# A decode step with paged attention: chosen-row copies at other places of a fixed order, and later places for some waits of ScalarE and VectorE

## The reference, cut to what matters

```
kc, vc  = compress(rows[:, :, 0]), compress(rows[:, :, 1])   # 255 compressed keys and values of 4096 cached rows
o_cmp,p = cmp_attention(q, kc, vc)                           # softmax over the 255
sel     = top_k(importance of 64 blocks from p, 16)          # per KV head, first and newest blocks forced
o_slc   = softmax(q . keys of the 16 chosen blocks) . values # 15*64+1 = 961 rows
o_win   = softmax(q . last 512 keys) . values
out     = g0*o_cmp + g1*o_slc + g2*o_win
```

## Time and profile before

| | |
|---|---|
| median of 3 runs | 2246.21 us (2242.72 to 2254.63) |
| the profiled execution | 2249.45 us, span 2247.6 us |
| TensorE matmuls (PE), busy | 2016.1 us, 90% of the span |
| VectorE (DVE) | 915.7 us, 41% |
| ScalarE (ACT) | 707.9 us, 31% |
| GpSimd (POOL) | 629.6 us, 28% |
| DMA | 247.86 MB, 110 GB/s on average |
| granted TensorE clock | 0.955 of full speed |

### The profile page before, as it was taken

The page is one execution under the profiler, slowest core; times in us unless marked ns, Lnnn a source line. Parts: engine busy times, 40 slices in busy tenths (PEclk is TensorE's granted clock), DMA queues, the critical chain, the costliest instruction groups (busy, mean ns, idle before and its releaser), DMA issues. The chain is left out here.

```text
span 2247.6 us, 24649 instructions
## 1 busy us (share of the span) xinstructions
PE 2016.1 (90%) x9303; PEld 1372.5 (61%) x9303; DVE 915.7 (41%) x1821; ACT 707.9 (31%) x1297; POOL 629.6 (28%) x649
## 2 busy tenths in 40 slices
PE   8999999999999999999968778677687878899997
PEld 7888888888888877777634334333343434434442
DVE  0445355454510144444434344445353545432126
ACT  0233112332200032332335444445354544510013
POOL 0000000000020034343545465555565555240000
PEclk9999999999999999999979889898888998999999
DMA  5232222222232211111155253545454453564114
GB/s 202 67 101 77 85 85 77 94 75 85 77 111 76 93 61 57 38 57 38 54 177 146 76 159 90 179 121 165 134 144 142 139 155 119 164 234 155 75 75 151
DMA packets 71076, 247.86 MB, mean 110 GB/s; under 512 B 11220, under 2 KB 28832, under 8 KB 56768
## 3 DMA queue, kind: packets, MB, share of 16 engines
q1 hardware_dynamic: 38344, 139.10, 17.8%
q0 software_dynamic: 31360, 103.32, 15.7%
q10 hardware_dynamic: 1280, 4.23, 0.5%
HBM read 224.64 MB, written 21.96 MB: 110 GB/s over the span
## 5 line engine op out<-in xcount | busy, mean ns | idle before, releaser
L292 PE MATMUL pj<-xT,strips 128*128 128x260 f32 x2368 | 532.6, 384 | 6.4 <-DMA xT<-d_xT 6.4
L292 PEld LDWEIGHTS pj<-xT,strips 128*128 128x128 f32 x2368 | 445.9, 191 | 72.3 <-issue 6.3
L1835 ACT ACTIVATE big<-dtb 64x512 f32<-64x512 f32 x512 | 302.8, 591 | 314.6 <-PE dtb L1569 172.2
L792 PE MATMUL pj<-xT,strips 128*128 128x260 f32 x1216 | 292.0, 388 | 0.0
L1592 PE MATMUL dpH<-big,w 128*128 128x512 f32 x512 | 287.3, 658 | 0.4 <-DVE hs L1958 0.4
L792 PEld LDWEIGHTS pj<-xT,strips 128*128 128x128 f32 x1216 | 222.4, 190 | 59.8 <-issue 30.1
L1018 POOL MEMSET kbd<- 128x128 f32 x1 | 0.2, 205 | 635.4 <-POOLq L126 635.4
L1569 PEld LDWEIGHTS dtb<-const,xT 128*128 128x128 f32 x512 | 65.3, 150 | 181.5 <-issue 87.5
L1941 DVE TENSOR_TENSOR big<-big 128x512 f32<-128x512 f32 x128 | 88.3, 689 | 212.5 <-ACT big L1835 174.2
L1569 PE MATMUL dtb<-const,xT 128*128 128x128 f32 x512 | 84.7, 292 | 99.9 <-DVE KgT L1807 79.2
L1044 POOL TENSOR_SCALAR old<-old,rd 128x128 f32<-128x128 f32 (+3 forms) x116 | 122.2, 1068 | 166.6 <-DVE rd L1153 166.6
(11 more groups left out here) (311 smaller groups left out, 2402.1 us busy)
## 6 DMA issues: line engine op xcount, KB each, us to landing
strips<-d_w_in SPq DMA_DIRECT2D x60, 1024.0 KB, 5.3
xT<-d_w_out SPq DMA_DIRECT2D x16, 1024.0 KB, 7.5
d_win_sample<-Wt SPq DMA_DIRECT2D x8, 1024.0 KB
Xr<-d_w_out SPq DMA_DIRECT2D x8, 1024.0 KB, 10.1
Wt<-d_win SPq DMA_DIRECT2D x8, 896.0 KB
xT<-d_xT SPq DMA_DIRECT2D x8, 520.0 KB, 8.9
Sold<-d_state SPq DMA_DIRECT2D x8, 512.0 KB, 5.5
vB<-v_rows ACTq DMA_DIRECT2D x8, 512.0 KB, 7.0
```

The source lines that it names most:

```text
L292: mm = nc.tensor.matmul(pj[b][:, a, 0:TH], w[b][:, k, :], xT[:, k, a * TH:(a + 1) * TH], start=(k == 0), stop=(k == KT - 1))
L792: mm = nc.tensor.matmul(bank(s)[:, n, 0:TH], w[s % 2][:, k, :], xT[:, k, n * TH:(n + 1) * TH], start=(k == 0), stop=(k == KT - 1))
L1835: ins = A(dst[:, :, :, hd], tb[bank][hd * DH:(hd + 1) * DH].rearrange("p (j h n) -> p j h n", j=2, h=2), ACT.Copy)
```

## The change

Two things are edited. In the table `AT` the four quarters' copies and their turns get other places; `LAST` stays as it is. And `program` takes a table `later` that shifts, for the engine that passes it, its own part of a piece by some places; the places themselves, from which banks are given out, are not shifted. ScalarE runs its three exponentials two places behind TensorE's scores. VectorE runs its copies of the second layer, the two maxima of `SCORES` and `WSCORES`, and `SUM` one place behind; its maximum of the compressed `scores` is not shifted. Where two pieces then meet at one place, the one that comes first in the table runs first. No instruction is added or removed.

```diff
-            ("second", 2): 51, ("second", 3): 53, "fetch0": 55, "mix": 56, "acc": 57, "keys0": 59,
-            "fetch1": 62, "keys1": 64, "fetch2": 70, "keys2": 71, "fetch3": 80, "keys3": 81,
+            ("second", 2): 51, ("second", 3): 53, "fetch0": 54, "keys0": 55, "mix": 56, "acc": 57,
+            "fetch1": 59, "keys1": 62, "fetch2": 66, "keys2": 70, "fetch3": 72, "keys3": 76,
...
-        def program(eng, do):
+        def program(eng, do, later={}):
 
+            due = {}
+            for t, (name, which) in pieces.items():
+                if name in do:
+                    due.setdefault(t + later.get(name, 0), []).append((name, which))
             for s in range(NSTEP):
                 for n in range(3):
                     do["product"](s, n)
                     then = unit(3 * s + n)
                     if then:
                         do["turn"](*then)
-                    name, which = pieces.get(3 * s + n, (None, None))
-                    if name in do:
+                    for name, which in due.get(3 * s + n, ()):
                         do[name](which)
...
-                name, which = pieces.get(3 * NSTEP + u, (None, None))
-                if name in do:
+                for name, which in due.get(3 * NSTEP + u, ()):
                     do[name](which)
...
-                **{FETCH[q]: fetch(q) for q in range(4)}})
+                **{FETCH[q]: fetch(q) for q in range(4)}}, {"scores": 2, "SCORES": 2, "WSCORES": 2})
...
-                "WSCALE": newest_scaled, "SUM": add_up, "DONE": done, **{FETCH[q]: fetch(q) for q in range(4)}, **key_pieces(V)})
+                "WSCALE": newest_scaled, "SUM": add_up, "DONE": done, **{FETCH[q]: fetch(q) for q in range(4)}, **key_pieces(V)},
+                {"second": 1, "SCORES": 1, "WSCORES": 1, "SUM": 1})
```

## The result

| | before | the change |
|---|---|---|
| median | 2247.27 us (2242.72 to 2254.63, 4 runs) | 2286.97 us (2284.15 to 2292.75, 4 runs) |
| ratio | | 1.0177, 95% interval 1.0142 to 1.0211 |
| profiled execution | 2249.45 us, span 2247.6 | 2285.88 us, span 2284.0 |

The account below looks back on a forecast made before the run. Bound: TensorE, busy 75 in 100 during the eight cached sequences, its idle time there being the change's worth. -21 - 15 + 3.5 = -33 us from the profiled 2249.45 us; predicted median 2214 us, range 2178 to 2264.

Parts of the forecast that it names:

- the term of the burst: 12 us TensorE stop before place 72 (24 within a sequence): 3.5 us saved in six sequences, -21 us.
- The gain of the burst: GpSimd's 6.4 us idleness before quarter 3's gathers goes, taking their 10 us out of the stop; ends 6.4 us or nothing.
- Rival (1): 16-gather run costs 5 us or more, places 66 and 68 late, X rows and window still meet; 2266 us, chance 0.2.
- The sign that I gave against it: During quarter 3's gathers in the old kernel TensorE was busy 8.9 of 9 us, half of their time.
- Quarter 3's keys: Copy and turn move from places 80 and 81 to 72 and 76; TensorE's 2.15 us wait goes, 7 times 2.2, -15 us.
- the marks set: In the changed profile: GpSimd's wait for VectorE's values copy under 15 us, TensorE's for ScalarE's key copies under 10.
- Quarter 0's turn after one place: One place between copy and turn instead of four; might bring a wait of 0 to +2.2 us, taken as 0.
- The exponentials' zero: ScalarE's exponential of the chosen scores two places later: ends -2 and +1.3 us per sequence, taken as 0.
- The scratch tile's wait at place 72: Quarter 3's copy waits for VectorE's product reading the shared tile: 0.5 us, +3.5 us over seven sequences.
- Rival (3): Quarter 3's rows not there at place 72; up to 5 us per sequence gives back the gain; 2248 us, chance 0.12.
- Rival (2): Window and X rows alone make the 12 us stop, which stays; only quarter 3's key wait is won; 2234 us, chance 0.2.

Follow-up runs that it names:

- chip 11: Later session; the unaltered change timed again beside the kernel before (2240.45 us): 2269.77 us, ratio 1.0136.
- chip 7: Session with the parts alone against the kernel before (2142.20 us); only the copies' and turns' new places, nothing shifted: 2134.82 us, ratio 0.9967.
- the fastest kernel: New places of copies and key turns, no later places, GpSimd waits behind quarters 2 and 3, against the kernel before: 2221.90 us, 0.9925; again 2234.30 us, 0.9921.

## Why the prediction was wrong

**The step that failed** is the term of the burst, "6.4 less 3, some 3.5 us saved" (-21 us). It was the sum's only term for late results, and it priced them in one run of gathers alone: "So 16 gathers cost between nothing and 7.5 us; I take 3, nearer to the 13." Place 17 shows 9.8 us more than before in the first measurement and 7.1 on chip 11, where on chip 7 the same table gives 1.3. Less this 1.3, the late increments cost 5.8 to 8.6 us per sequence: two to three times the value taken, and on both sides of its upper bound. The bound came from one wait of the first sequence, in whose run of 21 the records now show updates up to 9.6 us late; the wait alone was read, not how long the releasing work had been done. The row of 13 gathers, towards which I leaned, was busy 5.4 of 7 us and held an update by 5.8 us.

**The gain of the burst** was mis-sized the other way: "the whole 6.4 us saved, or nothing". Place 24 lost 12.5 us, of which 1.9 are the table's on any chip (3.4 to 1.6 on chip 7) and some 10 the stop. So what was saved at one place outweighs what the run of 16 took at the other by some 2 us, of the 3.5 forecast.

**What decides the sign is what the sum put at nothing: the other runs of gathers.** On the chips without late increments a sequence takes 92 us with either table (change with a wait behind quarter 2: 92.0; later places only: 92.2). Measured from there, late increments cost the kernel before some 14 us per sequence and the change some 20.5. The two stops are 10.4 of the one and 8.6 of the other; the rest rose from some 3 to some 12 us. Places 14, 37, 42 and 45 alone take 7 us more per sequence than before, where on chip 7 the table adds 0.5. Gathers run beside them, X rows and quarter 0, in runs that the new order shaped anew; how much each run's length gives was not tested one by one, but the kernel with a wait behind quarter 3 shows how much such a run can cost.

**Rival (1)** has the mechanism, its place and its sign: the long run holds TensorE. Its second half is so in part: the X rows start late (GpSimd waits 102.9 us for TensorE's turns, 64.3 before) and still meet the window, but without a stop there. Its own 2266 us was also low. The sign that I gave against it, that quarter 3's gathers ran half of their time beside a busy TensorE, proved nothing: a run holds little in its first ten microseconds or so, and those rows showed just these. And the burst does not end "when the DMA engines run empty": its update comes at 1629.31, with the DMA share at 0.95 in that microsecond.

**Right.** Quarter 3's keys: 15 us were forecast; the place lost 3.7 us, 1.3 of it the turn that moved, so 2.4 us times seven is 17. On chip 7 TensorE's key waits fell by 16.5, though the whole table gained only 7.4 us there. GpSimd's wait for VectorE's copy and TensorE's for the key copies fell below the marks set (none, and 4.4 us). The still stretch before place 72 is gone (place 24 takes 1.3 us in all), under 10 as the mark had it. Quarter 0's turn after one place brought no wait that shows: on chip 7 place 7 gains the moved turn's 1.4 us and place 11 loses 1.0. The exponentials' zero holds at 2142 us (0.9994), where it is made of +20.7 and -20.4. It does not hold at 2240, where the later places alone cost 0.55%; which of them does it was not separated.

**Smaller misses.** The scratch tile's wait at place 72 (+3.5 us) does not appear: no row has ScalarE's quarter-3 copy wait for VectorE. It was worth 0. Rival (3), rows not there at place 72, fell: place 24 takes 1.3 us. The window copies that were to hold these rows back came only at 1631.06, 15 us behind the end of quarter 3's traffic, so nothing here tests them beside it. Rival (2) fell with the change itself, in which window and X rows meet without a stop, and with the kernels that made the stop without a window copy. "Sequences take about 101 us" was 112.5; the second still stretch at the end of quarter 3's gathers is the mark that the prediction named for being wrong.

The late increments and the rule that I set against them: on the chips at 2142 us no increment was late and 16 gathers beside TensorE cost nothing. The Trainium skill (SBUF — State Buffer, "Who interferes with whom") has it that a DMA never contends with a compute engine and that TensorE never waits on anyone; it says so of the ports of SBUF. The traces of both kinds of chip agree with that much: beside the 16 gathers of the change TensorE's matmuls follow each other every 0.43 us at 1609 us, as elsewhere at the full clock. What is late on the slower chips, up to 19 us at one place, is the update behind finished work, of which the rule says nothing. So it could not settle the burst's term, and a forecast with this term at 0 (2234 us) would have been wrong as well.

**What stays open.** Why some chips do this and others don't: the program, the gathers' pace (one per 1.25 us on each) and the DMA traffic are the same. Whether it is the gathers' transfers or GpSimd's own work of issuing them that holds the increments; a wait stops both. (In four stops the release comes 1.1 to 3.8 us after the last gather was issued, at a DMA share of 0.00 in two and of 0.75 and 0.95 in the others, which speaks against the amount of traffic.) Whether the tracing has a part: every time on record comes with a traced span, and the chips with late increments are also those whose traces miss update records (9,300 to 10,100 in all, against 14,800 on the chips at 2142 us); no run here was made without a trace. Why the later places cost 0.55% at 2240 us is open too. The unaltered change was timed on no chip of the 2142 kind, only its two parts and itself with a wait (0.9967, 0.9994, 0.9973 and 0.9979), and the fastest kernel on none either.

## What to carry to other kernels

A wait that is shortened on an engine which issues gathers joins two runs; count the length of every run of gathers before and after, and read from the trace not only who waited but how long ago the releasing instruction had ended. Where ends and increments lie apart, breaking a run with a wait until it has landed can be worth more than the idle time that it costs, but in the right places only: three kernels here moved the stop elsewhere, and waits behind every eight X rows cost 2% where nothing was late. A verdict of 1 or 2% should be taken on more than one chip: the table alone was 0.9967 on one and 1.0074 on another.

## What the runs showed of the hardware

- The same kernel takes 2142 us on two chips and 2239 to 2249 us on the others, 4.5% more. In the traces nearly all of it lies in the cached sequences: 106 us each in the kernel before on a slower chip, 92 us on a chip of the other kind in the kernels nearest to it.
- On the slower chips TensorE's semaphore updates come late, up to 19 us, while GpSimd issues gathers without a pause. The first ten microseconds of a run (eight gathers) hold little: TensorE is busy 10.3 us of 11 from 1629 to 1640 us in the fence above, 3 to 14 us into a run. The last held update arrives 1.1 to 3.8 us after the last gather of the run was issued; in the change three arrive together, within 0.14 us.
- The DMA share alone doesn't decide it: the stops stand at a DMA share of 0.17 and less (the change), 0.33 (quarters 0 to 2) and 0.72 (X rows), while at 0.94 to 0.97 with window copies TensorE worked 10.5 us of 16 and 12.9 of 17.
- A stop lowers TensorE's clock: granted 0.58 on average in the stop of 12 us and 0.64 in the 16 us behind the change's stop, and 1.00 ahead of both. In the change it is at the lower of its two levels (1.2 of 2.4 GHz) from 1614.77 to 1628.42, and matmuls of one product start 0.85 us apart there, 0.43 ahead of it. So a part of a stop's price is paid in slower products after it.
